# Working off a tile's 128 expert slots in two parts of 64, with a shorter first round of the triangular inverse and earlier output stores

## The chip, the cores and the metric

The kernel runs on one core of a Trainium2 chip. The metric is device time in microseconds, the median over runs. The kernel before took 4612.51 us (three runs, 4605.46 to 4624.1).

## What is computed

One inference step of a two-layer decoder trunk, for a prompt of 512 tokens (four tiles of 128) and eight sample sequences with one token each. In each layer three token mixers (windowed attention, gated DeltaNet, stick-breaking attention) share one input projection and one output projection. After them comes a mixture of single-neuron experts (PEER): eight heads pick 16 of 16384 experts each, so that every token has 128 slots.

```
    def expert_block(args):
        xk, ik, gk = args
        act = jax.nn.gelu(jnp.einsum('nd,ned->ne', xk, u_tab[ik]).astype(jnp.float32), approximate=False)
        return jnp.einsum('ne,ned->nd', (gk * act).astype(v_tab.dtype), v_tab[ik])
```

For each slot of each token one row of 1024 floats of the table `peer_u` is fetched and multiplied with the token's vector (a dot), and one row of `peer_v` is fetched and added with the weight gate times GELU(dot).

The DeltaNet mixer needs the inverse of a unit lower triangular 128x128 matrix per head and tile:

```
    t_inv = lax.linalg.triangular_solve(eye + m_low, jnp.broadcast_to(eye, m_low.shape),
                                        left_side=True, lower=True)
```

## The kernel before, in words

**Windows.** The prompt is cut into units of two tiles in one layer: unit 0 and 1 are layer 0, unit 2 and 3 layer 1. The token mixers of a unit must precede its experts. After a first window for the modulation and a second one for the mixers of unit 0 there are four *expert windows*: in the first the experts of unit 0 run beside the mixers of unit 1, in the second the experts of unit 1 beside the mixers of unit 2, in the third the experts of unit 2 beside the mixers of unit 3, in the fourth the experts of unit 3 beside the mixers of the samples. The first begins, and the fourth ends, with a small batch of the samples (16 steps of dots, 16 of rows). Each window is one block; a barrier stands between two.

**Steps.** `experts` writes the work of a window down as a list of steps. A step of kind "u" is a slot's dots: GpSimd issues an indirect DMA that gathers 128 rows of `peer_u`, 4 KB for each partition (L2457), and VectorE multiplies and adds them up (L2507). A step of kind "v" is a slot's rows: the same with `peer_v`, and then either TensorE adds the gathered tile to two PSUM banks through a diagonal matrix of the weights (L2561; the diagonal is made by ScalarE, L2544) or VectorE adds it to `ACC` (L2521, L2523). `on_dve` says which: never the first eight rows, then one in four (`ON_DVE`), or one in two (`ON_DVE_ALONE`) for the last tile of the last window. The gathers go through a ring of 12 buffers, `G_`; a gather waits until its buffer's last user is done.

**Order of the steps.** `phases` gives it. For a unit with tiles a and b it is: all 128 dots of a; then a's 128 rows alternating with b's 128 dots; then b's 128 rows. This makes 512 steps. Below an *eighth* is 64 of these steps. Eighths 1 and 2 are dots alone, 3 to 6 are mixed, 7 and 8 are rows alone. Between a tile's last dot and its rows stands a chain: VectorE signals `dots_done` (L2510), ScalarE applies GELU (L2535, with a load of its function table), VectorE multiplies by the gate (L2514), ScalarE makes diagonals, TensorE starts. Three steps after a tile's last row `flush` adds banks and `ACC` to `X` (L2478 to L2495).

**Merge.** The mixers are stages (norm, project, unit_lengths, heads, attend_a, attend_c, delta_chunks, delta_inverse, delta_scan, gated_norm, out_projection, norm, queries, choose_tile twice), each with a length by hand (`paced`). `when` gives each of their ticks a fraction of the window, the n-th expert step has the fraction n/steps, and `window` sorts all by it. In this one order every engine's program is written; an engine executes its own in order. So a mixer tick stands at a fixed expert step, whatever the steps contain. Each stage ends in a barrier of four engines (L2340). `choose_tile` (L308 to L386) is nearly all VectorE work.

**Inverse.** `delta_inverse` has LEVELS (7) times two tiles = 14 rounds. A round is: VectorE masks (L1429), TensorE multiplies (L1399), ScalarE copies (L1413), TensorE multiplies twice (L1391, L1392), VectorE subtracts twice (L1422, L1423). R and T begin as identities that ScalarE writes (L1407, L1408).

**Stores.** The last block writes all of `y_prompt` (L2679) and `y_sample` (L2680) and waits for both.

## Time and profile before

| | |
|---|---|
| median of 3 runs | 4612.51 us |
| the profiled execution | 4607.17 us, span 4605.0 us |
| first to last gather of the four expert windows | 942.6 to 1872.3, 1888.9 to 2712.5, 2729.0 to 3595.2, 3615.6 to 4553.4 us |
| VectorE / TensorE busy | 2877.4 / 3316.4 us |
| granted TensorE clock, mean | 0.84 of full speed |

The granted clock is given in parts of full speed: 1.00 is 2.4 GHz, 0.50 is 1.2 GHz. A row with x8 stands for eight instructions. L numbers are lines of the kernel before.

### The profile page before, as it was taken

How to read it: one execution, taken by the hardware profiler on the slowest of the kernel's cores; microseconds unless marked ns; L12 is line 12 of the kernel's file. 1: busy time of each engine (PE TensorE's matmuls, PEld its weight loads, DVE VectorE, ACT ScalarE, POOL GpSimd, SP SyncE). 2: the span in 40 equal slices, each digit the busy share in tenths (PEclk: the TensorE clock that was granted, in tenths of full speed). 3: DMA queues.
4: the chain of work that ended last, by engine and by line, in shares of the span. 5: the costliest groups of instructions: out<-in, count | busy, mean ns of one | idle time of the engine just before them, and what ended most of it. 6: DMA issues, size and time to landing. Idle time of an engine off the chain costs nothing. (4 is left out here: it accounts for less than half of the span.)

```text
span 4605.0 us, 41650 instructions
## 1 busy us (share of the span) xinstructions
PE 3316.4 (72%) x11670; PEld 1851.6 (40%) x11670; DVE 2877.4 (62%) x5807; ACT 864.2 (19%) x2031; POOL 2596.9 (56%) x2244
## 2 busy tenths in 40 slices
PE   6945868847298789575888967698888334568776
PEld 2523653326155553352555425455553111223321
DVE  1236355638857639797764687877628787774353
ACT  1123110011242122113321221252122001011110
POOL 0026300036777657687775666777546687676573
PEclk8965978869599899787998988899999657888896
DMA  5524345469989989899998889999979799999895
GB/s 210 176 86 138 115 128 169 170 161 362 345 324 357 342 320 349 329 408 344 381 384 311 308 315 381 376 350 351 342 274 338 276 317 369 386 396 392 322 364 153
DMA packets 557775, 1372.36 MB, mean 298 GB/s; under 512 B 66986, under 2 KB 258739, under 8 KB 556348
## 3 DMA queue, kind: packets, MB, share of 16 engines
q0 software_dynamic: 306176, 1107.44, 65.1%
q1 hardware_dynamic: 232940, 245.48, 16.0%
q10 hardware_dynamic: 18432, 16.79, 1.1%
q8 instruction: 98, 1.61, 0.1%
q14 instruction: 129, 1.06, 0.1%
HBM read 1357.75 MB, written 11.95 MB: 297 GB/s over the span
## 5 line engine op out<-in xcount | busy, mean ns | idle before, releaser
L2457 POOL DMA_INDIRECT arena<-in_peer_u_dram,arena x1056 | 1280.4, 1212 | 861.9 <-POOLq L2452 475.2
L2561 PE MATMUL bank<-arena 128*128 128x512 f32 (+1 forms) x3144 | 1538.0, 636 | 240.0 <-PEq L2558 118.9
L2457 POOL DMA_INDIRECT arena<-in_peer_v_dram,arena x1056 | 1169.4, 1107 | 726.6 <-PE bank L2561 410.5
L2507 DVE CUSTOM_DVE_ANT_0 arena<-arena 128x1024 f32<-128x1024 f32 (+1 forms) x1056 | 1266.4, 1224 | 427.7 <-DMA arena<-in_peer_u_dram,arena 397.6
L2561 PEld LDWEIGHTS bank<-arena 128*128 128x128 f32 (+1 forms) x3144 | 588.8, 196 | 1034.6 <-issue 821.0
L2544 ACT ACTIVATE arena<-arena 128x128 f32<-128x128 f32 (+1 forms) x786 | 289.0, 394 | 1068.4 <-PE bank L2561 708.3
L2523 DVE SCALAR_TENSOR_TENSOR arena<-arena 128x1024 f32<-128x1024 f32 x262 | 336.4, 1284 | 244.0 <-DMA arena<-in_peer_v_dram,arena 228.4
L2184 POOL DMA_INDIRECT arena<-in_cache_sb_k_dram,arena x64 | 83.3, 1302 | 331.5 <-POOLq L2177 304.6
L817 PE MATMUL bank<-arena 128*128 128x256 f32 (+1 forms) x1024 | 245.0, 400 | 15.5 <-PEq L807 15.4
L817 PEld LDWEIGHTS bank<-arena 128*128 128x128 f32 x1024 | 202.6, 200 | 59.2 <-issue 28.8
L644 PE MATMUL bank<-arena 128*9 128x512 f32 x384 | 188.4, 650 | 31.0 <-PEq L642 17.7
L811 PE MATMUL bank<-arena 128*128 128x264 f32 (+1 forms) x768 | 176.9, 392 | 12.8 <-PEq L807 12.7
L1599 PE MATMUL bank<-arena 128*128 128x256 f32 (+1 forms) x640 | 154.1, 399 | 38.4 <-PEq L1597 38.4
L811 PEld LDWEIGHTS bank<-arena 128*128 128x128 f32 x768 | 148.4, 195 | 43.9 <-issue 20.7
L723 PE MATMUL bank<-arena 128*128 128x128 f32 (+1 forms) x160 | 33.6, 377 | 169.3 <-PEq L719 169.3
L1599 PEld LDWEIGHTS bank<-arena 128*128 128x128 f32 (+1 forms) x640 | 114.7, 180 | 86.5 <-issue 59.0
L2213 PE MATMUL bank<-arena 128*4 128x256 f32 x512 | 118.9, 387 | 16.4 <-PEq L2162 14.6
L1681 PE MATMUL bank<-arena 128*128 128x256 f32 x512 | 119.1, 389 | 4.8 <-PEq L1677 4.7
L933 PE MATMUL bank<-arena 128*128 128x256 f32 x64 | 31.8, 649 | 119.3 <-PEq L931 119.3
L1681 PEld LDWEIGHTS bank<-arena 128*128 128x128 f32 x512 | 99.6, 196 | 29.8 <-issue 16.6
L644 PEld LDWEIGHTS bank<-arena 128*9 128x9 f32 x384 | 35.7, 96 | 171.4 <-issue 170.8
L723 PEld LDWEIGHTS bank<-arena 128*128 128x128 f32 (+1 forms) x160 | 28.0, 216 | 182.3 <-issue 182.2
(345 smaller groups left out, 3777.9 us busy)
## 6 DMA issues: line engine op xcount, KB each, us to landing
arena<-in_w_in_dram SPq DMA_DIRECT2D x52, 1024.0 KB, 12.4
arena<-in_w_ada_dram SPq DMA_DIRECT2D x24, 2048.0 KB, 9.8
arena<-in_w_out_dram SPq DMA_DIRECT2D x24, 1024.0 KB, 15.4
arena<-in_peer_wq_dram SPq DMA_DIRECT2D x24, 1024.0 KB, 16.5
arena<-in_peer_u_dram,arena POOLq DMA_INDIRECT x1056, 6.9
arena<-in_peer_v_dram,arena POOLq DMA_INDIRECT x1056, 6.2
arena<-in_cache_sb_k_dram SPq DMA_DIRECT2D x128, 128.0 KB, 3.9
arena<-in_cache_sb_v_dram SPq DMA_DIRECT2D x128, 128.0 KB, 4.7
```

Source lines behind the costliest of these rows:

```text
L644: last = pe_.matmul(ps[n % 2][0:R9, 0:width], CT[:, k, :], W[n % ring][:, k, :], start=(k == 0), stop=(k == KD - 1))
L811: last = pe_.matmul(ps[t % BANKS][:, 0:wide], m.W[c % ring][:, k, off:off + P], m.HT[:, k, 0:wide], start=(k == 0), stop=(k == KD - 1))
L817: last = pe_.matmul(ps[t % BANKS][0:r, 0:hi - lo], m.HT[:, k, i * P:i * P + r], m.W[c % ring][:, k, 0:hi - lo], start=(k == 0), stop=(k == ...
L1599: last = pe_.matmul(bank(g)[0:r, 0:CW_], m.OT[:, k, i * P:i * P + r], m.W[j % ring][:, k, 0:CW_], start=(k == 0), stop=(k == KD - 1))
L1681: last = pe_.matmul(ps[h % 3][:, 0:n_], m.W[h // 2 % ring][:, k, (h % 2) * P:(h % 2 + 1) * P], m.HT[:, k, 0:n_], start=(k == 0), stop=(k = ...
L2184: pool_.indirect_dma_start(m.HALF[h % 4][:, j, :], None, rows, bass.IndirectOffsetOnAxis(ap=m.IDP[:, at:at + 1], axis=0)).then_inc(paged[h ...
L2213: last = pe_.matmul(ps[b % 2][0:NH, 0:AW], weights[:, half * HP + j, :], m.HALF[n % 4][:, j, :], start=(half == 0 and j == 0), stop=(half ...
L2457: pool_.indirect_dma_start(G_[g % GR][0:b.parts, :], None, tables[0 if which == "u" else 1], bass.IndirectOffsetOnAxis(ap=b.index[:, n:n + ...
L2507: vec.tensor_tensor_reduce(row, row, b.h, 1.0, 0.0, ALU.mult, ALU.add, b.AV[0:b.parts, n:n + 1]).then_inc(freed_by_dve, 1)
L2523: i_ = vec.scalar_tensor_tensor(ACC, G_[g % GR], b.AV[:, n:n + 1], ACC, ALU.mult, ALU.add)
L2544: act_.activation(DG[order % NDG][0:b.parts, 0:b.rows], b.mark, ACT.Copy, scale=b.AV[0:b.parts, mine:mine + 1]).then_inc(diag_ready, 1)
L2561: last = pe_.matmul(ps[6 + i][0:b.rows, :], DG[owners[g][1] % NDG][0:b.parts, 0:b.rows], G_[g % GR][0:b.parts, i * GBLK:(i + 1) * GBLK], s ...
```

## The change

A tile's 128 slots are worked off in two parts of 64 (`PART`). The order for a unit is now: dots of a's first part; rows of it alternating with dots of a's second part; rows of that alternating with dots of b's first part; rows of that alternating with dots of b's second part; rows of b's second part. The number of steps, 512, and the steps at which mixer ticks stand are the same. Eighth 1 is dots alone, 2 to 7 are mixed, 8 is rows alone. GELU, gate and the signals of the chain work on 64 columns, once for each part, four times in a unit instead of twice; the flush of tile a falls behind eighth 5 instead of eighth 6. One row in two goes to VectorE only in the second part of the last prompt tile.

In the inverse the first level no longer multiplies with identities: TensorE transposes the masked matrix, and VectorE writes identity minus that into R and identity minus the mask into T. The four ScalarE copies of the identity, the ScalarE copy of a round and the two products of a round are gone for two of 14 rounds.

`y_prompt` is stored tile by tile, two steps after each tile's flush in layer 1, in SyncE's program of the window; the last block stores `y_sample` alone.

```
+PART = 64
+def ends(b, n):
+    first = n // PART * PART
+    return first, min(first + PART, b.n)
...
 def on_dve(b, n):
-    return not b.sample and n >= FIRST_ON_DVE and n % b.every == b.every - 1
+    every = ON_DVE_ALONE if b.alone and n >= b.n - PART else ON_DVE
+    return not b.sample and n >= FIRST_ON_DVE and n % every == every - 1
...
-                        if t >= 4 and t % 2 == 0 and n < len(rounds):
+                        if t >= 4 and t % 2 == 0 and nt <= n < len(rounds):
...
+                            if v == 0:
+                                for h in range(NH):
+                                    last = pe_.transpose(ps[n % 2][:, hs(h)], m.LM[n % 2][:, hs(h)], ident)
+                                last.then_inc(pe2dve, 1)
...
-                        if t == 0:
-                            for i in range(nt):
-                                act_.copy(H4(m.R[:, i, :]), bc(ident, 1, NH))
-                                last = act_.copy(H4(m.T[:, i, :]), bc(ident, 1, NH))
-                            last.then_inc(act2dve, 1)
...
+                            if v == 0:
+                                vec.tensor_tensor(H4(m.R[:, i, :]), bc(ident, 1, NH), H4(ps[n % 2][:, :]), ALU.subtract)
+                                vec.tensor_tensor(H4(m.T[:, i, :]), bc(ident, 1, NH), H4(m.LM[n % 2]), ALU.subtract).then_inc(dve_own, 1)
...
-                rows = [((n + 1) / b.n, i, which, b, n) for i, (which, b) in enumerate(phase) for n in range(b.n)]
+                rows = [((n + 1 - first) / PART, i, which, b, n) for i, (which, b, first) in enumerate(phase) for n in range(first, ends(b, first)[1])]
...
+                    for done in batches:
+                        if done.l == DEPTH - 1 and not done.sample and step == min(done.flush_at + 2, steps - 1):
+                            sp_.wait_ge(added, done.turn + 1)
+                            sp_.dma_start(done.y, done.x).then_inc(stored, 16)
...
-                        if n == b.n - 1:
+                        if n == ends(b, n)[1] - 1:
                             vec.wait_ge(freed_by_dve, owners[g][1])
                             vec.sem_inc(dots_done, 1)
-                    if which == "v" and n == 1:
+                    if which == "v" and n == ends(b, n)[0] + 1:
                         vec.wait_ge(gelu_done, 1).then_inc(gelu_done, -1)
...
-                        while n >= 1 and b.diagonals < len(b.on_pe) and b.on_pe[b.diagonals] <= n + LEAD:
+                        while n > first and b.diagonals < len(b.on_pe) and b.on_pe[b.diagonals] <= min(n + LEAD, end - 1):
...
-            phases = [[("u", a)], [("v", a), ("u", b)], [("v", b)]]
+            halves = [(tile, first) for tile in (a, b) for first in range(0, SLOTS, PART)]
+            phases = [[("u", *halves[0])]] + [[("v", *before), ("u", *after)] for before, after in zip(halves, halves[1:])] + [[("v", *halves[-1])]]
...
-                sp.dma_start(outs["y_prompt"][0].rearrange("(t p) d -> p t d", p=P), X[:, 0:NT, :]).then_inc(stored, 16)
                 sp.dma_start(outs["y_sample"].rearrange("b s d -> (b s) d"), X[0:NB, NT, :]).then_inc(stored, 16)
-                sp.wait_ge(stored, 32).then_inc(stored, -32)
+                sp.wait_ge(stored, 16 * (NT + 1)).then_inc(stored, -16 * (NT + 1))
```

TensorE's program in the third expert window, at the end of the input projection (stage project), before. L817, L811 and L814 are the projection, L933 belongs to unit_lengths, L2561 is a slot's rows (two matmuls for each):

```order
1101 L814 MATMUL bank<-arena 8x256 x8
1102 L817 MATMUL bank<-arena 128x256 x16
...
1103 L817 MATMUL bank<-arena 128x256 x16
1104 L814 MATMUL bank<-arena 8x256 x8
1105 L933 MATMUL bank<-arena 128x256 x8
1106 L937 MATMUL bank<-arena 36x128
1107 L2561 MATMUL bank<-arena 128x512 x14
```

The same place in the changed kernel, where L826 and L823 are the projection, L942 unit_lengths and L2578 the rows:

```order
1119 L823 MATMUL bank<-arena 8x256 x8
1120 L2578 MATMUL bank<-arena 128x512 x2
1121 L826 MATMUL bank<-arena 128x256 x8
1122 L2578 MATMUL bank<-arena 128x512 x2
1123 L826 MATMUL bank<-arena 128x256 x8
1124 L2578 MATMUL bank<-arena 128x512 x2
1125 L823 MATMUL bank<-arena 8x256 x8
1126 L2578 MATMUL bank<-arena 128x512 x10
1127 L942 MATMUL bank<-arena 128x256 x2
```

Rows of tile a's first part now stand between the groups of the projection, where there were none.

VectorE's program in the second expert window, where the stage choose_tile 0 begins (L308, L313, L318 are its searches), before. L2523 is a row on VectorE:

```order
1274 L2523 SCALAR_TENSOR_TENSOR arena<-arena 128x1024 x3
1275 L308 MAX arena<-arena 128x8 x16
1276 L2523 SCALAR_TENSOR_TENSOR arena<-arena 128x1024
1277 L313 MAX_INDEX arena<-arena 128x8 x16
1278 L2523 SCALAR_TENSOR_TENSOR arena<-arena 128x1024
1279 L318 MATCH_REPLACE arena<-arena 128x128 x16
```

The same place in the changed kernel, where L317, L322 and L327 are the searches, L2538 a row on VectorE and L2521 a dot (its product and the reading of its sum):

```order
1245 L317 MAX arena<-arena 128x8 x16
1246 L2521 ISA arena<-arena 128x1024
1247 L2521 ISA arena 128x1
1248 L2521 ISA arena<-arena 128x1024
1249 L2521 ISA arena 128x1
1250 L322 MAX_INDEX arena<-arena 128x8 x16
1251 L2538 SCALAR_TENSOR_TENSOR arena<-arena 128x1024
1252 L2521 ISA arena<-arena 128x1024
1253 L2521 ISA arena 128x1
1254 L327 MATCH_REPLACE arena<-arena 128x128 x16
```

Dots of tile b's second part now stand between the searches.

SyncE's program at the end of the kernel, before:

```order
1347 L1643 DMA arena<-in_peer_keys_dram 128x2x64 x8
1348 L1646 DMA arena<-in_peer_wq_dram 128x8x256 x4
1349 L2468 DMA arena<-modulation 8x1024
...
1352 L2679 DMA out_y_prompt_dram<-arena 128x4x1024
1353 L2680 DMA out_y_sample_dram<-arena 8x1024
```

And in the changed kernel:

```order
1346 L2482 DMA out_y_prompt_dram<-arena 128x1024
1347 L2369 DMA arena<-in_w_out_dram 128x8x256 x4
1348 L1583 DMA arena<-modulation 8x1024
...
1351 L1658 DMA arena<-in_peer_wq_dram 128x8x256 x4
1352 L2482 DMA out_y_prompt_dram<-arena 128x1024
1353 L2478 DMA arena<-modulation 8x1024
...
1356 L2699 DMA out_y_sample_dram<-arena 8x1024
```

The prompt's tiles are stored inside the windows, the first of them ahead of the samples' w_out loads; only the samples' store stands in the last block.

## Rows read from the trace of the kernel before

**Rows 1.** The page: the span.

```profile
span 4605.0 us, 41650 instructions
```

**Rows 2.** Windows, all engines: the fastest stretch, and eighth 4 of window two.

```profile
core 0: us, PE busy (x) PEld busy (x) DVE busy (x) ACT busy (x) POOL busy (x), PEclk, DMA share, GB/s
2000.00:2050.00 50.00, 44.96 (x196) 37.57 (x194) 43.27 (x77) 6.20 (x20) 41.04 (x30) 0.97 1.04 405
...
2211.00:2301.00 90.00, 74.50 (x296) 44.62 (x295) 71.86 (x133) 23.47 (x69) 68.73 (x65) 0.91 0.99 377
```

**Rows 3.** Windows, all engines: eighth 2 of windows one to four.

```profile
1156.00:1259.00 103.00, 27.04 (x69) 15.00 (x69) 90.90 (x155) 20.23 (x42) 83.50 (x65) 0.50 0.94 347
...
2018.00:2111.00 93.00, 37.97 (x144) 30.03 (x144) 79.98 (x134) 12.70 (x23) 73.79 (x64) 0.67 0.99 389
...
2865.00:2963.00 98.00, 70.69 (x297) 47.04 (x295) 83.73 (x144) 13.86 (x30) 76.29 (x65) 0.84 0.97 376
...
3744.00:3856.00 112.00, 22.00 (x31) 7.44 (x31) 102.93 (x189) 4.09 (x9) 89.54 (x65) 0.50 0.98 356
```

**Rows 4.** Windows, all engines: eighth 7 of windows one to four.

```profile
1677.00:1794.00 117.00, 114.99 (x352) 57.61 (x350) 68.07 (x240) 26.64 (x69) 69.37 (x64) 1.00 0.84 297
...
2524.00:2633.00 109.00, 105.50 (x313) 50.23 (x312) 69.87 (x240) 26.05 (x67) 68.69 (x65) 1.00 0.87 307
...
3377.00:3508.00 131.00, 128.56 (x416) 70.83 (x417) 55.18 (x218) 30.16 (x79) 65.18 (x66) 0.97 0.83 291
...
4316.00:4429.00 113.00, 93.07 (x328) 48.55 (x328) 49.78 (x77) 20.75 (x56) 69.40 (x65) 0.94 0.94 339
```

**Rows 5.** Windows, all engines: stage queries of windows two and three.

```profile
2476.00:2559.00 83.00, 72.27 (x284) 46.54 (x284) 20.48 (x27) 16.79 (x42) 36.42 (x38) 0.92 0.84 296
...
3378.00:3457.00 79.00, 77.81 (x298) 48.49 (x299) 8.76 (x8) 17.96 (x49) 30.41 (x31) 0.96 0.76 259
```

**Rows 6.** Windows, all engines: stage choose_tile 0 of windows two and three.

```profile
2559.00:2638.00 79.00, 74.41 (x171) 32.27 (x172) 69.24 (x244) 17.81 (x45) 55.66 (x50) 1.00 0.91 330
...
3457.00:3532.00 75.00, 63.37 (x148) 27.37 (x146) 67.27 (x240) 14.26 (x35) 50.73 (x47) 0.97 0.88 317
```

**Rows 7.** Windows, line L2523 alone, on the first stretch of rows 6.

```profile
2559.00:2638.00 79.00, 14.45 (x12) 1.00 0.91 330
```

**Rows 8.** Timeline, VectorE, window two, eighth 2 into 3.

```profile
2108.57 0.08 DVE L2507 DVE_READ_ACCUMULATOR2_ANT arena<- 128x1 f32 x1
2108.97 1.23 DVE L2507 CUSTOM_DVE_ANT_0 arena<-arena 128x1024 f32<-128x1024 f32 x1 [0.32 <-DMA arena<-in_peer_u_dram,arena]
...
2110.72 0.28 DVE L2514 TENSOR_TENSOR arena<-arena 128x128 f32<-128x128 f32 x1
```

**Rows 9.** Timeline, all engines: TensorE's first rows just behind rows 8.

```profile
2111.83 5.30 PE L2561 MATMUL bank<-arena 128*128 128x512 f32 x8 [17.41 <-PEq L2558]
...
2117.39 5.39 PE L2561 MATMUL bank<-arena 128*128 128x512 f32 x12 [0.26 <-PEq L2558]
```

**Rows 10.** Timeline, VectorE, window two, eighth 6 into 7.

```profile
2509.28 0.08 DVE L2507 DVE_READ_ACCUMULATOR2_ANT arena<- 128x1 f32 x1
2520.07 1.28 DVE L2484 TENSOR_TENSOR arena<-arena,bank 128x512 f32<-128x512 f32 x2 [10.71 <-DVEq L2480]
...
2524.55 0.29 DVE L2514 TENSOR_TENSOR arena<-arena 128x128 f32<-128x128 f32 x1 [0.35 <-DVEq L2512]
```

**Rows 11.** Timeline, all engines: the inverse of unit 0, its first round.

```profile
487.68 1.29 DVE L1429 TENSOR_TENSOR arena<-arena 128x512 f32<-128x512 f32 x2 [5.50 <-DVEq L1427]
...
494.27 0.49 PE L1391 MATMUL bank<-arena 128*128 128x128 f32 x2
...
495.93 0.39 PE L1392 MATMUL bank<-arena 128*128 128x128 f32 x2
```

**Rows 12.** Timeline, the end: the samples' last rows, the prompt's store.

```profile
4539.35 54.77 PE L2561 MATMUL bank<-arena 64*8 64x512 f32 x64 [28.52 <-PEq L2558]
...
4597.68 0.40 SPq L2679 DMA_DIRECT2D out_y_prompt_dram<-arena  x1
```

More of the change, by code:

```diff
@@ L1397, in pe @@
                             pe_.wait_ge(dve2pe, 1).then_inc(dve2pe, -1)
-                            for h in range(NH):
-                                last = pe_.matmul(ps[n % 2][:, hs(h)], m.LM[n % 2][:, hs(h)], m.R[:, i, hs(h)], start=True, stop=True)
-                            last.then_inc(pe2act, 1)
+                            if v == 0:
+                                for h in range(NH):
+                                    last = pe_.transpose(ps[n % 2][:, hs(h)], m.LM[n % 2][:, hs(h)], ident)
+                                last.then_inc(pe2dve, 1)
+                            else:
+                                for h in range(NH):
+                                    last = pe_.matmul(ps[n % 2][:, hs(h)], m.LM[n % 2][:, hs(h)], m.R[:, i, hs(h)], start=True, stop=True)
+                                last.then_inc(pe2act, 1)
                         yield
@@ L1404, in act @@
                     for t in range(ticks):
-                        if t == 0:
-                            for i in range(nt):
-                                act_.copy(H4(m.R[:, i, :]), bc(ident, 1, NH))
-                                last = act_.copy(H4(m.T[:, i, :]), bc(ident, 1, NH))
-                            last.then_inc(act2dve, 1)
                         n = (t - 3) // 2
-                        if t >= 3 and t % 2 == 1 and n < len(rounds):
+                        if t >= 3 and t % 2 == 1 and nt <= n < len(rounds):
                             act_.wait_ge(pe2act, 1).then_inc(pe2act, -1)
@@ L2414, in experts @@
             for phase in phases:
-                rows = [((n + 1) / b.n, i, which, b, n) for i, (which, b) in enumerate(phase) for n in range(b.n)]
+                rows = [((n + 1 - first) / PART, i, which, b, n) for i, (which, b, first) in enumerate(phase) for n in range(first, ends(b, first)[1])]
                 walked += [row[2:] for row in sorted(rows, key=lambda row: row[:2])]
-            batches = [b for phase in phases for which, b in phase if which == "v"]
-            for phase in phases:
-                for which, b in phase:
-                    if which == "v":
-                        b.every = ON_DVE_ALONE if last and len(phase) == 1 else ON_DVE
+            batches = [b for phase in phases for which, b, first in phase if which == "v" and first == 0]
+            for b in batches:
+                b.alone = last and b is phases[-3][0][1]
             number = Walked.batches
@@ L2507, in dve @@
                         vec.tensor_tensor_reduce(row, row, b.h, 1.0, 0.0, ALU.mult, ALU.add, b.AV[0:b.parts, n:n + 1]).then_inc(freed_by_dve, 1)
-                        if n == b.n - 1:
+                        if n == ends(b, n)[1] - 1:
                             vec.wait_ge(freed_by_dve, owners[g][1])
                             vec.sem_inc(dots_done, 1)
-                    if which == "v" and n == 1:
+                    if which == "v" and n == ends(b, n)[0] + 1:
                         vec.wait_ge(gelu_done, 1).then_inc(gelu_done, -1)
-                        w = b.AV[0:b.parts, 0:b.n]
-                        vec.tensor_tensor(w, w, b.gate, ALU.mult).then_inc(dve_own, 1)
+                        part = slice(*ends(b, n))
+                        w = b.AV[0:b.parts, part]
+                        vec.tensor_tensor(w, w, b.gate[:, part], ALU.mult).then_inc(dve_own, 1)
                         vec.wait_ge(dve_own, 1).then_inc(dve_own, -1)
@@ L2531, in act @@
                     if which == "v":
+                        first, end = ends(b, n)
+                        if n == first:
+                            act_.wait_ge(dots_done, 1).then_inc(dots_done, -1)
+                            w = b.AV[0:b.parts, first:end]
+                            act_.activation(w, w, ACT.Gelu).then_inc(gelu_done, 1)
                         if n == 0:
-                            act_.wait_ge(dots_done, 1).then_inc(dots_done, -1)
-                            w = b.AV[0:b.parts, 0:b.n]
-                            act_.activation(w, w, ACT.Gelu).then_inc(gelu_done, 1)
                             b.diagonals = 0
-                        if n == 1:
+                        if n == first + 1:
                             act_.wait_ge(gated, 1).then_inc(gated, -1)
-                        while n >= 1 and b.diagonals < len(b.on_pe) and b.on_pe[b.diagonals] <= n + LEAD:
+                        while n > first and b.diagonals < len(b.on_pe) and b.on_pe[b.diagonals] <= min(n + LEAD, end - 1):
                             mine = b.on_pe[b.diagonals]
@@ L2628, in tile_batch @@
         def tile_batch(u, i):
-            return Batch(u.l, SLOTS, P, u.H[i], IDI[u.sets + i], GT[u.sets + i], ident, P, X[:, u.tiles[i], :], False)
+            b = Batch(u.l, SLOTS, P, u.H[i], IDI[u.sets + i], GT[u.sets + i], ident, P, X[:, u.tiles[i], :], False)
+            b.y = outs["y_prompt"][0].rearrange("(t p) d -> p t d", p=P)[:, u.tiles[i], :]
+            return b
         def sample_batch(l):
@@ L2673, in build @@
                 of_sample = [paced(LS.rows_back(samples[1], rooms[1][0]), 4)] + LS.token_mixers(samples[1], rooms[1])
-                window([], [(of_sample, 0.0, 0.8)], phases + [[("u", s)], [("v", s)]])
+                window([], [(of_sample, 0.0, 0.8)], phases + [[("u", s, 0)], [("v", s, 0)]])
         with nc.Block() as block:
```

10 lines of the change are left out of this document (5 added, 5 removed).

## Prediction, written before the changed kernel ran

> **What bounds the kernel now.** I read the span first [rows 1], then cut the four expert windows into their eighths (64 steps each, counted by the gathers' issues) and read what each engine and the transfers did in each. The change moves work only between eighths: eighth 2 turns from dots alone to mixed, eighth 7 from rows alone to mixed. The others keep their kind, so those two are shown for all windows [rows 3, 4].
>
> The ceiling of the transfers comes first. The fastest stretch moved 405 GB/s at a DMA share of 1.04 [rows 2]; I take 400 as what can be had for long. A mixed eighth, the fourth of window two, took 90 us for 64 gathers at 377 GB/s, with VectorE busy 72 us and TensorE 75 [rows 2]. Nothing is far from full there.
>
> Eighth 2 [rows 3] is a matter of VectorE and transfers: VectorE is busy 91 of 103, 80 of 93, 84 of 98 and 103 of 112 us, transfers run at 347, 389, 376 and 356 GB/s, and TensorE is busy 27, 38, 71 and 22 us. Window three's 71 is a projection that lasts longer there, since it carries the samples' columns.
>
> Eighth 7 [rows 4] looks at first like the opposite: TensorE busy 115 of 117, 105.5 of 109, 129 of 131, 93 of 113 us, at 297, 307, 291 and 339 GB/s. The reader is to see that it is not one stretch but two. In window two the stage queries holds TensorE 72 of 83 us and VectorE only 20 [rows 5]; in choose_tile 0 behind it VectorE is busy 69 of 79 us and TensorE 74 [rows 6]. Window three is alike: 78 of 79 with VectorE at 9, then VectorE 67 of 75 [rows 5, 6]. What helps the first stage loads the second.
>
> **Prices.** A dot is 1.23 us and the reading of its sum 0.08 [rows 8]: 1.3. A row on VectorE is 14.45/12 = 1.2 us [rows 7]. A row on TensorE is four matmul instructions: 5.39/12 x 4 = 1.8 us at full clock [rows 9], 54.77/64 x 4 = 3.4 at half clock, by the samples' last rows, which stand at the same width of 512 [rows 12].
>
> **Eighth 2** loses 32 dots and gains rows 0 to 31 of the same tile, of which n = 11, 15, ... 31 (six) fall to VectorE and 26 to TensorE. VectorE: -32 x 1.3 + 6 x 1.2 = -35 us. TensorE: +26 x 1.8 = +47 us. The bytes stay; by rate times length they are 35.7, 36.2, 36.8 and 39.9 MB, or 89, 90, 92 and 100 us at 400 GB/s [rows 3].
> Window one: VectorE 56, TensorE 74, transfers 89; I take 95, -8. Window two: 45, 85, 90; 93, no change. Window three: VectorE 49, TensorE 71 + 47 = 118, or 107 if the present 71 us at a clock of 0.84 became 60 at full clock; 110, +12. Window four: 68, 69, 100; 102, -10. Sum -6. I add 2 to 5 us to the largest of three because an engine's program is strictly in order and every row waits for its gather and its diagonal.
>
> **Eighth 7** loses 32 rows and gains 32 dots. In windows one to three 50 of its rows are on TensorE and 14 on VectorE; afterwards 24 and 8. By stage, with the share of steps that a stage's length gives it:
> Window two, queries: 21 of its 37 steps lie here. Before, 83 x 21/37 = 47 us. Afterwards TensorE has 21/37 of the stage's own work (72 less 21 rows x 1.8 = 34, so 19) and 8 rows, 33 us; transfers 296 GB/s x 47 us = 14 MB, 35 us; I take 37, -10 [rows 5].
> Window two, choose_tile 0: 43 of 55 steps. VectorE's own part is 69 - 14 = 55 us, 78% of it 43 us; with 21 dots (28) and 5 rows (6) it is 77 us, where the stage now takes 0.78 x 79 = 62 [rows 6, 7]. I take 80, +18. Net +8.
> Window one has 24 steps of queries and 40 of choose_tile 0; by the same sums -9 and +16, net +7.
> Window three has 33 steps of queries, 79 us now. TensorE: 78 less 26 rows x 1.8, 31 us, and 13 rows, 23: 54; transfers 20.5 MB, 51; I take 58, -21 [rows 5]. Of choose_tile 0 it has 29 steps of 48: VectorE 33 + 19 + 4 = 56 against 0.6 x 75 = 45 [rows 6], +12. Net -9.
> Window four has no choose stage, and its rows alone went half to VectorE. TensorE 93 - 15 x 1.8 = 66, VectorE 50 + 42 - 23 x 1.2 = 64, transfers 38.3 MB, 96: 99, -14 [rows 4]. Sum of eighth 7: -8.
>
> **Part boundaries.** Each unit gets four chains of GELU and gate instead of two. The plain one cost 2111.83 - 2108.65 = 3.2 us from the last dot to the first row, and VectorE lost about 2 us of dots [rows 8, 9]; the ring of 12 gathers covers some of it. The one with the flush of tile a cost 15 us from last dot to gate, 10.7 of them VectorE waiting at L2478 for TensorE, which stood in queries [rows 10]. Its flush now comes an eighth earlier, out of that stage: -5 over the windows. Eight more plain ones: between 0 (all under the ring) and 8 x 3.2 = 26; I take 12. At the end of eighth 7 it falls into choose_tile, where VectorE has nothing to spare; what queues behind the wait for GELU there are dots and searches. The worst bound is that a new one costs what the flush one does, 15 us.
>
> **Inverse.** In the first round TensorE's two products run from 494.27 to 496.1, 1.8 us [rows 11]; two rounds lose them, 3.6 us in each of four units. VectorE's start waits 5.50 us, 2 of which are the identity copies. The transposes replace the first product one for one. In unit 0 no experts run beside it and TensorE is nearly full, so -6; elsewhere they lie in eighth 5 beside transfers, -1.5 each. Sum -10, bounds 0 and -24.
>
> **Stores.** From the prompt's store to the end is 4605.0 - 4597.7 = 7.3 us [rows 1, 12]. The samples' 32 KB remain; I take 2.5 us for them, so -5; bounds 0 and -7. Moved into the windows, 2 MB are 5 us at 400 GB/s in the least, spread over two windows; SyncE's wait for the flush stands ahead of the w_out loads, for some us in one stage; I cost both at nothing.
>
> **Sum.** -6 - 8 - 5 + 12 - 10 - 5 = -22 us on the profiled 4607.2, so 4585. The runs' median is 5 us above that execution; I say 4587.
>
> **The rivals.**
> Clock. In eighth 2 the granted clock is 0.50, 0.67, 0.84 and 0.50 [rows 3], and in the mixed eighth it is 0.91 [rows 2]. I expect it to rise with the rows. Were it to stay, 26 rows at 3.4 us would be +89: TensorE 116, 127, 160 and 111 us against 103, 93, 98 and 112 now, +13 + 34 + 62 + 0, some +109 with the rest of the sum unchanged but its -6: about 4700. The Trainium skill (TensorE: Matmul & The Clock Gate, Part 1) says that sustained activity releases the throttle and an idle stretch brings it back; rows spread among waits for gathers could be too thin by that. The mixed eighth's 0.91 speaks against it.
> Choose. VectorE at the full load of choose_tile 0 falls behind in all three windows, and the relief in queries does not come because its ticks wait on barriers. Then +18 +16 +12 stay without -40: 4625. With each boundary in it like the flush one (+12 more in three windows) it is 4660. It decides from about 20 us of VectorE work too much per window. Speaks for it: 77 us of VectorE work where 62 us pass now.
> Nothing. Gains of some 20 us are eaten by boundaries: 4600 to 4612.
> Even. Each eighth goes to its largest load over all 64 steps, since the ring and the queues even out the two stages: eighth 7 gives 104, 106, 95 and 96 us, -69; eighth 2 gives 89, 90, 107 and 100, -20; with -20 for the rest: 4498.
> The DMA page of the Trainium skill (DMA: Bandwidth & Descriptors, Anatomy of one DMA) fits a software-issued DMA with 2.0 us and 436 GB/s, which is 1.2 us of streaming for one gather. By it the estimate for eighth 7 of window four would be 88 us instead of 96. The best stretch here moved less, 405 GB/s, and the sum goes by the rows.
>
> **How the numbers follow.** Change of 0.5% (23 us) is what can be told from none. The balanced sum holds 0.40; its own range is 4555 to 4615, so 0.24 of it is faster and 0.16 the same. Even, or half way to it: 0.20, faster. Nothing: 0.16, of which 0.13 the same and 0.03 faster. Choose: 0.15, slower. Clock: 0.04, slower. Boundaries like the flush one at all eight places, 15 less 1.5 each, +108 and so about 4690: 0.05, slower. That is 0.47, 0.29 and 0.24. The range reaches half way into the cases at either side: 4510 to 4655.
>
> **What would show it.** Right: eighth 2 of window one or four shorter with VectorE below 70 us busy, of window three longer with TensorE over 105; the clock in all of them above 0.8; queries shorter, choose_tile 0 at 95 to 100 us; the last store gone from the end. Wrong: a clock near 0.5 in eighth 2, choose_tile 0 under 85 us (then VectorE was not the limit), or gaps over 10 us at the new boundaries.

## The result, and the profile after

The changed kernel took 4658.41 us (median of three, 4646.45 to 4682.69) against 4612.51: ratio 1.010, 95% interval 1.0069 to 1.0131. It is slower by 46 us, where 25 us less were forecast. The profiled execution is the slowest of the three, 4682.69 us, 75.5 above that of before. Of such a difference between two single traces some 30 us belong to the execution; below it is said where most of them lie. All ratios below are of comparisons over several executions; the one of chains_ahead leaves out an execution of 18182 us, whose cause is open.

The page's span and its two largest groups on TensorE and VectorE (busy us, mean ns, idle us before them and what ended most of it). Line L2578 is L2561 of before, L2521 is L2507:

```profile
span 4680.8 us, 41512 instructions
...
L2578 PE MATMUL bank<-arena 128*128 128x512 f32 (+1 forms) x3200 | 1668.9, 667 | 409.5 <-PEq L2575 224.2
...
L2521 DVE CUSTOM_DVE_ANT_0 arena<-arena 128x1024 f32<-128x1024 f32 (+1 forms) x1056 | 1273.2, 1224 | 705.9 <-DMA arena<-in_peer_u_dram,arena 665.2
```

The dots now wait 665.2 us for their gathers, where the trace of before had 397.6. A slower transfer would show like this too, so the next question is who held the gathers back. Cut by the same gathers as before, the eighths took these times (us, before -> after). The cuts stand some 11 gathers behind the first of each eighth, about the depth of the ring, so in windows one to three the last eighth has only 53 gathers in it:

| eighth | window one | two | three | four | sum of the differences |
|---|---|---|---|---|---|
| 1 | 112 -> 114 | 129 -> 127 | 136 -> 137 | 129 -> 127 | -1 |
| 2 | 103 -> 102 | 94 -> 115 | 98 -> 128 | 112 -> 100 | +38 |
| 3 | 106 -> 100 | 99 -> 99 | 97 -> 103 | 112 -> 112 | 0 |
| 4 | 94 -> 94 | 90 -> 97 | 99 -> 103 | 122 -> 122 | +11 |
| 5 | 90 -> 92 | 89 -> 93 | 96 -> 97 | 119 -> 119 | +7 |
| 6 | 128 -> 119 | 134 -> 135 | 123 -> 137 | 108 -> 103 | +1 |
| 7 | 117 -> 119 | 109 -> 111 | 130 -> 126 | 112 -> 120 | +8 |
| 8 | 78 -> 88 | 80 -> 90 | 87 -> 91 | 91 -> 82 | +15 |

**Eighth 2** is where the loss is, and in windows two and three alone. The same windows view as in [rows 3], windows one to four:

```profile
1159.00:1261.00 102.00, 72.14 (x185) 32.26 (x183) 69.27 (x113) 28.34 (x69) 69.84 (x65) 0.87 0.93 352
...
2017.00:2131.00 114.00, 98.38 (x292) 58.97 (x292) 54.22 (x84) 23.73 (x59) 71.11 (x64) 0.91 0.91 328
...
2909.00:3037.00 128.00, 118.54 (x406) 67.98 (x405) 53.70 (x87) 28.42 (x70) 73.22 (x65) 0.95 0.84 289
...
3841.00:3941.00 100.00, 75.21 (x141) 28.80 (x140) 77.31 (x133) 13.28 (x36) 79.67 (x65) 0.83 1.02 389
```

The clock rose as forecast (0.87, 0.91, 0.95, 0.83) and VectorE's load fell to 54 us in windows two and three, and still the eighth is longer there. An eighth is too wide a cut here. The stretch of the input projection alone, after, in windows two and three:

```profile
2013.00:2081.00 68.00, 62.17 (x218) 42.95 (x219) 28.41 (x48) 14.85 (x41) 35.77 (x33) 0.92 0.90 323
...
2904.00:2999.00 95.00, 94.22 (x360) 58.56 (x359) 39.72 (x67) 18.31 (x54) 46.52 (x41) 1.00 0.84 285
```

And the same steps before:

```profile
2014.00:2063.00 49.00, 31.62 (x137) 26.61 (x135) 43.04 (x75) 3.93 (x11) 39.07 (x33) 0.87 1.04 409
2063.00:2111.00 48.00, 8.18 (x16) 4.69 (x16) 40.51 (x68) 9.10 (x12) 37.94 (x34) 0.50 0.96 370
2860.00:2926.00 66.00, 64.75 (x292) 44.88 (x291) 58.99 (x101) 8.00 (x25) 50.05 (x40) 1.00 1.01 386
```

In window three TensorE was busy 64.75 of 66 us at clock 1.00 already. The change put 68 matmul instructions there, 17 rows of 1.8 us or 30 us, and the stretch grew by 29. In window two it was busy 32 of 49 us, behind it 8 of 48; the rows filled the first stretch to 62 of 68, and it grew by 19 of the eighth's 21 us. The rest of the eighth went from 48 to 50.

How it looks there, in window two's timeline of TensorE, VectorE and GpSimd (start, us, idle before in brackets; L826 is the projection):

```profile
2044.15 3.60 PE L2578 MATMUL bank<-arena 128*128 128x512 f32 x8
2044.19 1.23 DVE L2521 CUSTOM_DVE_ANT_0 arena<-arena 128x1024 f32<-128x1024 f32 x1 [1.53 <-DMA arena<-in_peer_u_dram,arena]
...
2046.31 0.94 POOL L2467 DMA_INDIRECT arena<-in_peer_v_dram,arena  x1 [2.85 <-PE bank L2578]
...
2047.59 3.62 PE L826 MATMUL bank<-arena 128*128 128x256 f32 x16
...
2048.29 1.23 DVE L2521 CUSTOM_DVE_ANT_0 arena<-arena 128x1024 f32<-128x1024 f32 x1 [2.87 <-DMA arena<-in_peer_u_dram,arena]
...
2051.04 1.88 PE L2578 MATMUL bank<-arena 128*128 128x512 f32 x4
...
2052.76 3.62 PE L826 MATMUL bank<-arena 128*128 128x256 f32 x16
```

TensorE has no gap; VectorE waits before each dot. GpSimd waits 2.85 us for TensorE to free a buffer before it can issue a row's gather, and the dots' gathers stand behind it in the same queue and ring. So a full TensorE now holds back the dots too, where before, with dots alone in these steps, their buffers waited for VectorE alone. That this wait sets the time is tested below.

**Eighth 7** to be read beside [rows 4], windows one to four:

```profile
1666.00:1785.00 119.00, 70.71 (x216) 33.60 (x214) 93.79 (x289) 12.15 (x31) 73.11 (x65) 0.82 0.84 292
...
2555.00:2667.00 112.00, 64.35 (x181) 27.43 (x179) 93.44 (x288) 11.21 (x28) 75.20 (x66) 0.78 0.85 304
...
3477.00:3603.00 126.00, 81.96 (x286) 47.68 (x284) 84.56 (x274) 13.05 (x34) 73.48 (x65) 0.85 0.84 301
...
4398.00:4518.00 120.00, 95.14 (x279) 53.35 (x280) 61.70 (x118) 14.63 (x40) 72.92 (x65) 0.72 0.88 316
```

In windows one to three TensorE is relieved by 41 to 47 us and VectorE loaded by 24 to 29, and the time stays within 5 us. In window two these are the first searches of choose_tile 0 and of choose_tile 1 in VectorE's timeline, before:

```profile
2564.80 2.42 DVE L308 MAX8 arena<-arena 128x8 f32<-128x128 f32 x12 [5.47 <-SPq L2340]
...
2642.64 3.19 DVE L308 MAX8 arena<-arena 128x8 f32<-128x128 f32 x16
```

And after:

```profile
2582.61 3.19 DVE L317 MAX8 arena<-arena 128x8 f32<-128x128 f32 x16
...
2688.98 3.19 DVE L317 MAX8 arena<-arena 128x8 f32<-128x128 f32 x16 [8.59 <-SPq L2352]
```

So choose_tile 0 takes 106 us instead of 78 (in window three 94 instead of 76, part of either difference lies in eighth 8), and TensorE's work of queries runs over 58 us instead of 73 (60 instead of 71). What queries gave, choose_tile took.

**Eighth 8** had no price of its own: its work is the same as before, rows alone. Windows one and two, after (before, they took 78 and 80 us):

```profile
1785.00:1873.00 88.00, 80.23 (x180) 34.87 (x180) 70.80 (x243) 21.12 (x51) 57.54 (x53) 0.94 0.85 305
...
2667.00:2757.00 90.00, 81.13 (x183) 35.19 (x184) 72.09 (x249) 20.84 (x50) 55.62 (x54) 0.95 0.86 312
```

At its start, 2667 us, stands the new boundary, inside choose_tile 0. Timeline of window two, the chain from the last dot to the first row:

```profile
2669.21 1.22 DVE L2521 CUSTOM_DVE_ANT_0 arena<-arena 128x1024 f32<-128x1024 f32 x1
...
2670.60 1.28 ACT L2551 ACT_TABLE_LOAD   x1 [61.42 <-ACTq L2549]
...
2671.89 0.26 ACT L2551 ACTIVATE arena<-arena 128x64 f32<-128x64 f32 x1
2672.29 0.23 DVE L2529 TENSOR_TENSOR arena<-arena 128x64 f32<-128x64 f32 x1 [1.86 <-DVEq L2526]
...
2672.80 1.86 ACT L2561 ACTIVATE arena<-arena 128x128 f32<-128x128 f32 x6 [0.65 <-ACTq L2555]
...
2673.34 6.97 PE L2578 MATMUL bank<-arena 128*128 128x512 f32 x12 [28.91 <-PEq L2575]
```

The chain itself is short: 2.9 us from the last dot's sum to the first row. What is long is TensorE's idle time before it, 28.91 us. The reading is: VectorE, full of searches, brings the part's last dots late; ScalarE may not prepare diagonals ahead of the gate; so TensorE runs dry, its clock falls (the twelve matmuls take 6.97 us; at full clock it was 5.39 [rows 9]), and the rows have to be caught up. In window four, without choose_tile, the eighth is 9 us shorter, but the 91 us of before are that trace's: inverse_and_stores, in the same order there, took 83.

**The flush** of tile a landed at the head of eighth 6. Timeline of window three, all engines:

```profile
3338.61 1.28 DVE L2498 TENSOR_TENSOR arena<-arena,bank 128x512 f32<-128x512 f32 x2
...
3341.49 1.22 DVE L2507 TENSOR_TENSOR arena<-arena 128x1024 f32<-128x1024 f32 x1
...
3344.15 0.22 DVE L2529 TENSOR_TENSOR arena<-arena 128x64 f32<-128x64 f32 x1
...
3344.64 1.86 ACT L2561 ACTIVATE arena<-arena 128x128 f32<-128x128 f32 x6 [7.89 <-ACTq L2555]
...
3346.59 0.80 PE L1458 MATMUL bank<-arena 128*128 128x128 f32 x2 [9.34 <-ACTq L2351]
...
3350.17 2.98 PE L2578 MATMUL bank<-arena 128*128 128x512 f32 x4
...
3353.43 0.94 POOL L2467 DMA_INDIRECT arena<-in_peer_v_dram,arena  x1 [11.26 <-PE bank L2578]
```

The flush on VectorE, some 4 us, stands ahead of the gate (L2529). ScalarE waits 7.89 us for the gate, TensorE 9.34 us for a stage's barrier in which ScalarE stands, the first row is at a low clock (2.98 us) and GpSimd, whose ring is full, waits 11.26 us. The eight gathers here took 22.2 us instead of 12.0; in windows one and two 17.7 instead of 11.4 and 18.6 instead of 11.6. Where the flush stood before, at the head of eighth 7, eight gathers became shorter by 1.4, 4.6 and 5.7 us in windows one to three. In windows one and two another eight gathers in the same eighth became shorter by 15.1 and 12.3 us, so the eighth's sum hides it there.

**Inverse and stores.** The first round of the inverse in unit 0, to be read beside [rows 11], and the last store:

```profile
486.59 1.29 DVE L1441 TENSOR_TENSOR arena<-arena 128x512 f32<-128x512 f32 x2 [3.01 <-SPq L2352]
...
490.44 0.66 PE L1409 MATMUL bank<-arena 128*128 128x128 f32 x4
...
4678.73 0.30 SPq L2699 DMA_DIRECT2D out_y_sample_dram<-arena  x1
```

VectorE starts after 3.01 us of waiting instead of 5.50, and one group of transposes stands where three groups of products were. From the last store to the end of the span are 2.1 us instead of 7.3.

### The profile page after: what moved, and what is told of

It is laid out like the page before. It is cut to its first block and busy times, and to the rows that moved or that the text cites. A ratio compares the mean times of both kernels' runs of the same rounds, so it can differ in the third digit from the quotient of the medians.

```text
span 4680.8 us, 41512 instructions
## 1 busy us (share of the span) xinstructions
PE 3405.4 (73%) x11566; PEld 1873.1 (40%) x11566; DVE 2866.4 (61%) x5801; ACT 862.5 (18%) x2037; POOL 2589.3 (55%) x2244
## 5 line engine op out<-in xcount | busy, mean ns | idle before, releaser
L2578 PE MATMUL bank<-arena 128*128 128x512 f32 (+1 forms) x3200 | 1668.9, 667 | 409.5 <-PEq L2575 224.2
L2521 DVE CUSTOM_DVE_ANT_0 arena<-arena 128x1024 f32<-128x1024 f32 (+1 forms) x1056 | 1273.2, 1224 | 705.9 <-DMA arena<-in_peer_u_dram,arena 665.2
L2578 PEld LDWEIGHTS bank<-arena 128*128 128x128 f32 (+1 forms) x3200 | 624.8, 206 | 1261.1 <-issue 948.5
L2561 ACT ACTIVATE arena<-arena 128x128 f32<-128x128 f32 (+1 forms) x800 | 290.5, 393 | 1063.7 <-PE bank L2578 593.1
L2538 DVE SCALAR_TENSOR_TENSOR arena<-arena 128x1024 f32<-128x1024 f32 x248 | 318.3, 1284 | 127.0 <-DMA arena<-in_peer_v_dram,arena 111.2
L826 PE MATMUL bank<-arena 128*128 128x256 f32 (+1 forms) x1024 | 246.8, 400 | 9.9 <-PEq L816 9.9
L826 PEld LDWEIGHTS bank<-arena 128*128 128x128 f32 x1024 | 204.1, 201 | 59.6 <-issue 29.6
L1611 PEld LDWEIGHTS bank<-arena 128*128 128x128 f32 (+1 forms) x640 | 109.9, 172 | 56.4 <-issue 29.2
L1693 PE MATMUL bank<-arena 128*128 128x256 f32 x512 | 120.2, 393 | 10.0 <-PEq L1689 6.7
L732 PEld LDWEIGHTS bank<-arena 128*128 128x128 f32 (+1 forms) x160 | 27.5, 213 | 182.9 <-issue 182.8
L669 DVE TENSOR_TENSOR arena<-bank,arena 9x512 f32<-9x512 f32 x24 | 16.3, 679 | 130.8 <-DVEq L668 74.5
```

Source lines behind the costliest of these rows:

```text
L826: last = pe_.matmul(ps[t % BANKS][0:r, 0:hi - lo], m.HT[:, k, i * P:i * P + r], m.W[c % ring][:, k, 0:hi - lo], start=(k == 0), stop=(k == ...
L1611: last = pe_.matmul(bank(g)[0:r, 0:CW_], m.OT[:, k, i * P:i * P + r], m.W[j % ring][:, k, 0:CW_], start=(k == 0), stop=(k == KD - 1))
L1693: last = pe_.matmul(ps[h % 3][:, 0:n_], m.W[h // 2 % ring][:, k, (h % 2) * P:(h % 2 + 1) * P], m.HT[:, k, 0:n_], start=(k == 0), stop=(k = ...
L2521: vec.tensor_tensor_reduce(row, row, b.h, 1.0, 0.0, ALU.mult, ALU.add, b.AV[0:b.parts, n:n + 1]).then_inc(freed_by_dve, 1)
L2538: i_ = vec.scalar_tensor_tensor(ACC, G_[g % GR], b.AV[:, n:n + 1], ACC, ALU.mult, ALU.add)
L2561: act_.activation(DG[order % NDG][0:b.parts, 0:b.rows], b.mark, ACT.Copy, scale=b.AV[0:b.parts, mine:mine + 1]).then_inc(diag_ready, 1)
```

## The experiments

Three theories were on record against each other before the first experiment. P: the loss is made where rows came into stages full on TensorE (the projection, eighth 2). D: it is made where dots came into choose_tile, full on VectorE (eighths 7 and 8). C: the two extra chains of GELU and gate in each unit cost it, wherever they stand. The kernels differ in a table that gives each window an order of its parts:

```
ORDERS = ('halves', 'halves', 'halves', 'halves')     # as in the change
def order_of(name, a, b):
    h, w = PART, 2 * PART
    if name == "whole":       # as before
        return w, w, [[("u", a, 0, w)], [("v", a, 0, w), ("u", b, 0, w)], [("v", b, 0, w)]]
    if name == "chains":
        return h, h, [[("u", a, 0, w)], [("v", a, 0, w), ("u", b, 0, w)], [("v", b, 0, w)]]
    if name == "early":
        return h, w, [[("u", a, 0, h)], [("v", a, 0, h), ("u", a, h, h)], [("v", a, h, h), ("u", b, 0, w)], [("v", b, 0, w)]]
    if name == "late":
        return w, h, [[("u", a, 0, w)], [("v", a, 0, w), ("u", b, 0, h)], [("v", b, 0, h), ("u", b, h, h)], [("v", b, h, h)]]
```

The first two values are the sizes in which the chain works for tile a and b. Each ratio is to the kernel before, run on the same chip (its medians there: 4612.3, 4609.4 and 4609.9 us).

### The change cut into its independent parts

inverse_and_stores is the kernel before with the new inverse and stores alone.

```
-ORDERS = ('halves', 'halves', 'halves', 'halves')
+ORDERS = ('whole', 'whole', 'whole', 'whole')
```

> The kernel before with the short first round of the inverse and the early stores, and the old order of steps. The three theories of the loss all put it in the order of steps: P, rows on TensorE inside the projection of windows two and three; D, dots on VectorE inside choose_tile; C, the two extra GELU chains of each unit. By all three this one gains what the prediction said of these two edits, 10 to 15 us against the kernel before. The rival: the stores block SyncE ahead of weight loads, or the inverse's added wait costs more than the products; then it is slower than before by 10 us or more.

Measured 4606.6 us, ratio 0.998 (0.9968 to 0.9994): -6 us, where the prediction had -15 and the expectation 10 to 15 less.

parts_alone is the other half: the parts, with the old inverse and stores.

> The new order of steps with the old inverse and the old stores. If the edits add up, it is some 60 us slower than before (the 46 us of the whole change and the 10 to 15 that the other edits give). If the loss came from the stores or the inverse, it is within 20 us of before.

Measured 4667.6 us, 1.0105 (1.0082 to 1.0127): +55. The two add up to +49, the change to +46. So the whole loss is the parts'. Its eighths repeat the change's within a few us: eighth 2 is 120 and 129 us in windows two and three, eighth 8 is 88 and 90 in one and two, eighth 6 is 136 in three.

chains_alone keeps the order of dots and rows of before and only works the chain twice for each tile.

```
+ORDERS = ('chains', 'chains', 'chains', 'chains')
```

> The kernel before with the old order of steps, but GELU, gate and their signals once for each 64 slots, four chains in a unit, as in the changed kernel. Theory C (the chains themselves cost): 30 to 60 us slower than before. Theories P and D (the chains are dear only where the order puts them): within 10 us of before, since at a part's middle its dots have long been done.

Measured 4627.0 us, 1.0035 (1.0020 to 1.0050): +15, between what C (30 to 60) and what P and D (within 10) had expected. The steps did not move, and yet eighth 8 takes 88, 88 and 91 us in windows one to three. That is the size of the loss in eighth 8 without a single dot in choose_tile.

### The projection taken out

parts_in_one_and_four has the parts only where no projection stands in eighth 2, with the new inverse and stores.

```
+ORDERS = ('halves', 'whole', 'whole', 'halves')
```

> New inverse and stores, the new order of steps in expert windows one and four, the old one in two and three. By the two traces the changed kernel lost 44 and 55 us in windows two and three, nothing in one, and gained 17 in four. Theory P (only windows two and three have much of their projection in eighth 2) expects 20 to 35 us less than before. Theory C, a cost for each chain in each window, expects no gain: within 15 us of the run with inverse and stores alone, or above it.

Measured 4582.2 us, 0.9936 (0.9912 to 0.9959): faster than before by 30 us, as P expected (20 to 35). Its eighth 2 takes 101 and 98 us in windows two and three. The parts gain in window four (eighth 2 is 100 us instead of 112); in window one the whole window takes the same time in both orders.

parts_in_four leaves them to window four alone.

```
+ORDERS = ('whole', 'whole', 'whole', 'halves')
```

> New inverse and stores, and the new order of steps in window four alone. By the sums of eighths window one gains in eighth 6 what it loses in eighth 8, so this is within 8 us of parts_in_one_and_four (4582). If the new order itself helped in window one, it is 15 us or more above it.

Measured 4585.6 us, 0.9946 (0.9923 to 0.9969), within the 8 us expected. The intervals of the two overlap: window one gives nothing that can be told.

### One half at a time

early_half cuts tile a alone (rows in the projection, no dots in choose_tile), late_half tile b alone. Both have the old inverse and stores.

```
+ORDERS = ('early', 'early', 'early', 'early')
```

> Old inverse and stores. Only tile a is cut into parts: eighth 2 and 3 mix a's rows with its own second part's dots, then a's second part goes with all of b's dots, one row to two dots; eighths 7 and 8 are b's rows alone, as before. It moves work into the projection and none into choose_tile. Theory P: most of the loss of the new order is here, eighth 2 of windows two and three again 20 and 30 us longer with TensorE over 95 us busy, and the whole 20 to 50 us slower than before. Theory D: within 15 us of before.

> Old inverse and stores. Only tile b is cut: eighths 1 and 2 are a's dots alone, as before; eighths 3 to 5 have two of a's rows to one dot of b's first part; 6 and 7 mix b's first rows with its second dots; 8 is rows alone. It moves dots into queries and choose_tile and no rows into the projection. Theory D: TensorE idles 20 us or more ahead of eighth 8, which is again 10 us longer, and the whole is 20 to 40 us slower than before. Theory P: within 15 us of before, or faster.

Measured: early_half 4666.3 us, 1.0117 (1.0090 to 1.0145), late_half 4675.3, 1.0128 (1.0098 to 1.0158). That is +57 and +66 us, beyond what either theory gave its own half (20 to 50 and 20 to 40), and each theory had the other half within 15. This was a miss: late_half is slow with no row in the projection. Here is eighth 2 of early_half, windows two and three:

```profile
2019.00:2136.00 117.00, 97.63 (x294) 58.29 (x292) 53.98 (x84) 23.93 (x59) 70.93 (x65) 0.91 0.90 323
2889.00:3018.00 129.00, 118.44 (x401) 66.76 (x400) 54.16 (x89) 28.91 (x71) 71.47 (x65) 0.95 0.82 283
```

It is the change's eighth 2 to 3 us, so that theory's mechanism and size stand. But an odd cut brings costs of its own. In early_half each row of a's second part meets two dots of b; eighths 4 and 5 of window two are 104 and 97 us (before 90 and 89), eighth 4 of window four 137 (122). In late_half each dot of b meets two rows: eighth 5 is 98 us in windows one and two (90 and 89). And late_half has the two boundary costs in full: eighth 8 is 88 and 90 us in windows one and two, and eighth 6 of window three, to be set beside the 123 us of before, is

```profile
3334.00:3472.00 138.00, 98.81 (x369) 65.41 (x370) 72.70 (x117) 27.31 (x59) 68.57 (x65) 0.87 0.82 299
```

Tile a's flush falls behind eighth 5 in late_half and in the change, behind eighth 6 in early_half (119 us) and parts_in_one_and_four (121). So the 14 us go with the flush's place. One loss of late_half is explained by none of this and stays open: eighth 2 of window two, whose steps are those of before, takes 106 us instead of 94.

### Is it the load of TensorE in the projection?

dense_rows_in_eighth_two is the changed kernel in which VectorE, idle half of that time, takes one row in two of these 32 (16 instead of 6).

```
+    if b.dense and n < PART // 2:
+        return n % 2 == 1
...
+            a.dense = k in (1, 2)
```

> The changed kernel, but in windows two and three one in two of tile a's rows 0 to 31 is on VectorE, from row 1 on: 16 rows instead of 6. TensorE loses 10 rows of 1.8 us in eighth 2, VectorE gains 10 of 1.3. Theory P (TensorE holds eighth 2 there and VectorE has room): eighth 2 of windows two and three 10 to 18 us shorter each, the whole 20 to 35 us faster than the changed kernel, near 4630. If transfers or the waits of VectorE for the gathers held it: no change, 4650 to 4660, or slower.

Measured 4633.9 us, 1.0053 (1.0021 to 1.0086), 24 below the change. Eighth 2 of windows two and three:

```profile
2011.00:2114.00 103.00, 78.30 (x252) 49.47 (x250) 65.81 (x93) 21.66 (x52) 72.51 (x64) 0.90 0.95 367
2893.00:3009.00 116.00, 103.62 (x371) 61.41 (x369) 66.43 (x97) 25.72 (x61) 69.31 (x64) 0.94 0.88 317
```

TensorE lost 20 and 15 us of work, the eighths 11 and 12. Nothing else was changed, and eighth 8 stayed at 90: TensorE's load is what lengthens eighth 2. Both sizes are within what P had expected.

### Is it the lead of the diagonals in eighth 8?

chains_ahead is chains_alone with GELU and gate six rows ahead of the part's end, so that ScalarE can prepare diagonals across the boundary.

```
-                    if which == "v" and n == ends(b, n)[0] + 1:
+                    if which == "v" and n in (1, b.part + 1 - AHEAD):
...
-                        while n > first and b.diagonals < len(b.on_pe) and b.on_pe[b.diagonals] <= min(n + LEAD, end - 1):
+                        while n > 0 and b.diagonals < len(b.on_pe) and b.on_pe[b.diagonals] <= n + LEAD:
```

> As chains_alone, but GELU, gate and signals of a tile's second 64 slots stand six steps of rows earlier in the programs, so that ScalarE can make diagonals ahead as in the kernel before. Chains_alone was 0.35% slower than before, with eighth 8 of windows one and two 8 to 10 us longer. If the loss there is the lead of the diagonals, which waits for a gate queued behind choose_tile on VectorE: eighth 8 back at 78 to 82 us and the whole within 8 us of before. If the table load or the extra instructions cost it: still 10 us or more slower than before.

Measured 4607.2 us, 0.9995 (0.9981 to 1.0009): the +15 of chains_alone are gone. Eighth 8 of window two, first chains_alone, then chains_ahead:

```profile
2649.00:2738.00 89.00, 81.02 (x182) 35.12 (x183) 72.62 (x248) 19.30 (x48) 56.98 (x55) 0.95 0.90 326
```

```profile
2631.00:2711.00 80.00, 73.79 (x168) 30.63 (x167) 70.97 (x246) 16.78 (x42) 57.87 (x53) 1.00 0.95 357
```

VectorE's work is the same; the clock is 1.00 again and the stretch 9 us shorter. The chain's work costs nothing that can be told; its place in the queues cost the 8 us. The run moves two things at once, the gate ahead in VectorE's queue and ScalarE's diagonals across the boundary, and does not part them. In the changed order this repair can't be made so: the part's last dots are themselves there only at the boundary. That the loss of eighth 8 is the same one there rests on its equal size and on TensorE's 28.91 us; no run repairs it in that order.

### A better version

Where queries keeps TensorE full [rows 5], rows can go to VectorE instead of dots being brought in. more_on_vector_in_queries is parts_in_one_and_four with, in windows two and three, one row in two on VectorE for tile b's rows inside that stage.

```
+    if 3 <= n < b.dense_to:
+        return n % 2 == 1
...
+            b.dense_to = (0, 22, 36, 0)[k]
```

> As parts_in_one_and_four, and in windows two and three, which keep the old order, tile b's rows from 3 on go one in two to VectorE as long as they stand in the stage queries (to row 21 and to row 35). There TensorE is full (72 of 83 and 78 of 79 us) and VectorE nearly idle. TensorE loses 7 and 10 rows of 1.8 us. If the load per stage sets the time: eighth 7 of windows two and three 8 to 15 us shorter each, and the whole 15 to 25 us below parts_in_one_and_four's 4582. If the waits of VectorE for gathers queue in front of the mixers, or transfers hold it: within 10 us of 4582.

Measured 4558.4 us, 0.9887 (0.9868 to 0.9906), 24 us below parts_in_one_and_four (15 to 25 expected) and the best of all here. Eighth 7 of windows two and three, before 109 and 130 us:

```profile
2537.00:2636.00 99.00, 94.61 (x284) 45.02 (x283) 78.71 (x247) 22.94 (x60) 72.04 (x65) 0.98 0.93 340
3389.00:3503.00 114.00, 111.68 (x379) 63.23 (x380) 67.09 (x227) 26.40 (x69) 67.55 (x64) 0.98 0.91 329
```

## Why the prediction was wrong

**Eighth 2, -6: this term failed.** It came out at +38 by the profiles. By windows: one -8, measured -1; two 0, measured +21; three +12, measured +30; four -10, measured -12. The step that failed is "TensorE 71 + 47 = 118, or 107 if the present 71 us at a clock of 0.84 became 60 at full clock; 110". The 0.84 was a mean over the eighth. In the 66 us of the projection the clock was already 1.00 and TensorE full, so nothing could shrink, and each row there was added to the end: 118.5 us busy, 128 long. For window two "VectorE 45, TensorE 85, transfers 90; 93" compared TensorE's 85 us with the whole eighth; it came to 98, and 62 of these stand in the stretch that took 49 us before. The prediction had cut eighth 7 into its two stages for just this reason, and did not do so with eighth 2. In window one the sum of loads gave 95 and the eighth stayed at 102, with no engine over 73 us and 352 GB/s. What holds it there stays open.

**Eighth 7, -8: about right** for windows one to three: +7, +8, -9, measured +2, +2, -4. As forecast, what queries gives is taken by choose_tile, whose stage 0 was to be at 95 to 100 us and took 106 and 94 in windows two and three. Window four, -14, depends on the clock (last section): 120 us in this trace, 100 to 106 in four of the experiments that have the same program there.

**Part boundaries, +12: near in size by luck, wrong in mechanism.** chains_alone adds eight chains and nothing else, though not all at the changed kernel's steps, and measured +15. But a boundary was priced by the length of its chain, 3.2 us each, partly hidden. The chain was indeed 2.9 us. Those inside choose_tile, where ScalarE loses its lead behind a full VectorE, cost 4 to 10 us each (eighth 8 of windows one to three, +10, +10, +4), and in chains_alone the other chains together cost nothing that can be told. The text had named this place, "where VectorE has nothing to spare", and then taken no price from it.

**The flush, -5: wrong in sign** by these rows. It saved 1.4 to 5.7 us where it left, and cost 6.3, 7.0 and 10.2 us where it came. Eighth 5's end was taken as free because it lies outside queries; it holds another stage's barrier.

**Inverse and stores, -15: right in kind, measured -6** (-3 to -15 by the interval). The store's 5 us are seen in the trace, so the inverse gave about nothing that can be told.

**The rivals.** Clock fell: 0.83 to 0.95 in eighth 2. The prediction had held it possible, beside the Trainium skill (TensorE: Matmul & The Clock Gate, Part 1), that rows spread among waits are too thin to release the throttle; these rows do not bear that out. Choose had the side and, by luck, the size (4625 to 4660), and half of the mechanism: VectorE in choose_tile was full, but it paid in eighth 8, by the chain, and 38 us came from the projection that no rival named. Nothing fell with the time, clear of before. Even fell: stages did not even out. Boundaries like the flush one at all eight places (4690) fell too: chains_alone put all eight at +15. Of what would show it wrong, gaps over 10 us at new boundaries did appear (28.91 and 11.26 us).

**The sum again**, with measured terms in windows one to four, by the profiles: eighth 2 +38, eighths 4 and 5 +18, eighth 8 +15, eighth 7 +8, the rest 0. This makes +79, against +75.5 of the two executions and +46 of the medians. The 18 us of eighths 4 and 5 are in part a lucky trace of before: eighth 4 of window two took 90 us there and 92 to 95 in four runs in the same order. 16 us of window four are the clock's. In eighth 8, on the other side, window four's -9 is a slow stretch in the trace of before (91 us, in inverse_and_stores 83); windows one to three alone give +24.

## What to carry to other kernels

Before moving work beside other work, cut the trace at the stages into which it moves, not at the unit in which it is counted, and add loads inside each: a stretch where one engine is busy 65 of 66 us at full clock takes nothing for free, whatever the mean around it. Price a new dependency chain not by its length but by what stands ahead of it in each in-order queue, and by the lead that the consumer loses; if it can be issued a few steps early it may cost nothing. When one engine is full and another idle in the same stage, changing which engine does the same work (one row in two instead of one in four) may be worth more than moving work: here it took the ratio from 0.9936 to 0.9887, where reordering all the work had lost 1.0%.

## What the runs showed of the hardware

One stretch of window four has two speeds. Its TensorE program is the same in the changed kernel and in parts_in_one_and_four. Here it is in the changed kernel by the windows view, and the timeline's group of TensorE that opens it:

```profile
4418.00:4458.00 40.00, 40.00 (x126) 27.47 (x126) 15.45 (x22) 1.60 (x5) 19.04 (x18) 0.53 0.73 240
```

```profile
4407.18 1.94 PE L1757 MATMUL bank<-arena 128*128 128x128 f32 x8 [14.15 <-PEq L1755]
```

And in parts_in_one_and_four:

```profile
4310.00:4333.00 23.00, 23.00 (x138) 17.13 (x137) 11.62 (x17) 2.00 (x6) 17.03 (x17) 1.00 0.98 357
```

TensorE is busy all the time in both, and the group that opens it stands behind an idle time of some 14 us in both; once it was granted 1.2 GHz for nearly the whole stretch, once 2.4, and 17 us lie between them. The slow form came in the changed kernel, parts_alone and parts_in_four, the fast one in four other runs, with 100 to 106 us for eighth 7 instead of 117 to 120. What decides is open. It makes single traces of these kernels differ by 16 us where the programs do not, and may be part of the spread of parts_in_one_and_four (4556 to 4600 us), of which only one execution was traced. So orders that differ by less are told apart by medians over several executions and not by single traces.
